# A two-layer hybrid decoder step: indexer keys loaded page by page by SyncE, K and V in one gather, weights and state laid out on the host

## The reference

```python
# per layer
z = h @ w_in                      # h = RMSNorm_pre(x); [q | k | v | indexer q | indexer k | head weights | pool input]
# indexer: relu(qi . ki) * wi, summed over 8 heads; the 256 (prompt: 128) best keys of each query stay
ki_past = cki[page_table].reshape(B, past, IDX_DIM)
_, sel = lax.top_k(sc, topk)
o = sparse_attend(q, k[sel], v[sel], valid)
p = pool(...)                     # running means over 2, 4, 8, 16 tokens, then a small matmul per group
x = x + RMSNorm_post(concat([o, p]) @ w_out)
x = x + RMSNorm_post(ConvGatedFFN(RMSNorm_pre(x)))     # gate and value 1024 x 2816, conv over 3 tokens, down
```

## Time and profile before

| | |
|---|---|
| median of 3 timed runs | 1708.46 us (1699.88 to 1721.88) |
| span of the profiled execution | 1881.7 us |
| PE busy | 1567.8 us, 83% |
| DVE, ACT, POOL busy | 45%, 26%, 14% |
| DMA | 116.45 MB, mean 62 GB/s |

### The profile page before, as it was taken

The page is one execution under the profiler, slowest core; times in us unless marked ns, Lnnn a source line. Parts: engine busy times, 40 slices in busy tenths (PEclk is TensorE's granted clock), DMA queues, the critical chain, the costliest instruction groups (busy, mean ns, idle before and its releaser), DMA issues.

```text
span 1881.7 us, 29237 instructions
## 1 busy us (share of the span) xinstructions
PE 1567.8 (83%) x10216; PEld 1330.8 (71%) x10216; DVE 850.0 (45%) x1731; ACT 482.0 (26%) x867; POOL 272.5 (14%) x260
## 2 busy tenths in 40 slices
PE   5369967748979999999862999766698999999996
PEld 3146644426969999999830758543487999998996
DVE  1003875624375555642210268753334655557221
ACT  4011301313342222332120132023234322224221
POOL 3710020150020000000176002004102000000002
PEclk8579977657989999999965996957678999999997
DMA  5112101010223333323311211011002233332331
GB/s 163 53 59 59 24 6 53 6 41 1 68 57 90 90 93 95 92 77 93 97 46 44 82 24 23 6 54 32 15 23 68 68 90 92 94 92 73 93 96 46
DMA packets 189622, 116.45 MB, mean 62 GB/s; under 512 B 25716, under 2 KB 184908, under 8 KB 189306
## 3 DMA queue, kind: packets, MB, share of 16 engines
q1 hardware_dynamic: 183246, 102.50, 19.7%
q0 software_dynamic: 6272, 12.63, 2.4%
HBM read 111.30 MB, written 4.44 MB: 62 GB/s over the span
## 4 chain that ended last, share of the span: by engine, by line
PE 72%; issue 12%; DVE 7%; ACT 3%; another core or an unknown queue 2%; DMA 1%; POOL 1%; DVEq 1%; SPq 0%; ACTq 0%; POOLq 0%
PE ps L740 44%; PE ps L725 6%; PE ps L765 4%; PE ps L837 3%; PE ps L984 2%; PE ps L1005 2%; PE ps L828 2%; PE ps L993 1%; POOL xT L620 1%; PE ps L854 1%; PE ps L712 1%; PE ps L788 1%; PE ps L1031 1%; DVE TS L1451 1%
## 5 line engine op out<-in xcount | busy, mean ns | idle before, releaser
L740 PE MATMUL ps<-moR_r,W_r 128*128 128x260 f32 x1408 | 284.8, 284 | 0.0
L740 PEld LDWEIGHTS ps<-moR_r,W_r 128*128 128x128 f32 x1408 | 219.0, 190 | 0.0
L620 POOL TENSOR_TENSOR xT<-xT,moR 128x520 f32<-128x520 f32 x32 | 45.6, 1462 | 1031.9 <-DVE moR L1468 1031.9
L740 PE MATMUL ps<-hT_r,QZC_r 128*128 128x260 f32 x896 | 183.9, 287 | 0.0
L725 PE MATMUL ps<-hT,W 128*128 128x260 f32 x576 | 163.4, 431 | 0.0
L765 PE MATMUL ps<-W,hT 128*128 128x328 f32 (+1 forms) x160 | 81.2, 609 | 94.5 <-issue 91.6
L740 PE MATMUL ps<-moR_r,QZC_r 128*128 128x260 f32 x704 | 148.5, 293 | 12.1 <-DVE hT_r L1810 11.8
L740 PE MATMUL ps<-moR_r,SQ_r 128*128 128x260 f32 x704 | 143.7, 285 | 0.0
L740 PEld LDWEIGHTS ps<-hT_r,QZC_r 128*128 128x128 f32 x896 | 142.4, 194 | 0.0
L740 PE MATMUL ps<-hT_r,SQ_r 128*128 128x260 f32 x704 | 141.4, 282 | 0.0
L765 PEld LDWEIGHTS ps<-W,hT 128*128 128x128 f32 (+1 forms) x160 | 33.4, 223 | 139.3 <-issue 129.4
(11 more groups left out here) (328 smaller groups left out, 3063.0 us busy)
## 6 DMA issues: line engine op xcount, KB each, us to landing
W<-in_w_gate SPq DMA_DIRECT2D x44, 512.0 KB, 3.9
W<-in_w_val SPq DMA_DIRECT2D x44, 512.0 KB, 3.9
W<-in_w_down SPq DMA_DIRECT2D x16, 1408.0 KB, 7.0
W<-in_w_in SPq DMA_DIRECT2D x8, 1024.0 KB, 5.6
W<-in_w_in SPq DMA_DIRECT2D x16, 256.0 KB, 4.2
W<-in_w_out SPq DMA_DIRECT2D x16, 256.0 KB, 4.1
W<-in_w_out SPq DMA_DIRECT2D x8, 512.0 KB, 5.1
yR<-in_x_prompt SPq DMA_DIRECT2D x1, 2048.0 KB
```

The costliest lines, as they stand in the source:

```text
L620: nc.gpsimd.tensor_tensor(xT[:, k, :], xT[:, k, :], mo[:, k, :], ALU.add).then_inc(x_ready.sem, 1)
L740: last = mm(ps[:, 2 * (g % 2) + f, 0:HT], w(k), x(k)[:, f * HT:(f + 1) * HT], start=(k == 0 and n == 0), stop=(k == nk - 1 and n == 2))
```

## The change

Indexer keys: the host lays the cache out as `idx_pages`, each page 64 dimensions by 128 keys. SyncE reads a page id from the page table in SBUF into a register and loads the page with a plain DMA (64 partitions by 128 floats). PE multiplies it directly; the page transposes on PE and the copies on ACT are gone, and so are POOL's 64 gathers per layer. K and V are one array `kv_rows` of 256 floats per row, fetched by 16 gathers per layer and not 32. Weights, x, y, the vectors and the convolution state are laid out by the host, so that each weight tile is one contiguous DMA and nothing is transposed at the start and the end. POOL copies the kept convolution columns in place of PE's transposes. The loop over the layers is written out.

```diff
-                wait_alone(sp, *so_ev(l, 0))
...
-                wait_alone(sp, *tile_done(l, 0))
-                load(0)
-                load(1)
+                if l:
+                    wait_alone(sp, *tile_done(l, 0))
+                    load(0)
+                    load(1)
+                with sp.Fori(0, NB) as b:
+                    for j in range(NPG):
+                        page = sp.value_load(PT[0:1, bass.ds(b, 1), j:j + 1], min_val=0, max_val=N_PHYS - 1)
+                        g = j % 2
+                        sp.dma_start(IK[64 * g:64 * g + 64, bass.ds(b, 1), j // 2, :],
+                                     A["idx_pages"][l, bass.ds(page, 1)].rearrange("o d r -> d o r")
+                                     ).then_inc(pages_in.sem, 16)
                 wait_alone(sp, *kv_mm(l, 5))
                 load(2)
```

```diff
             def layer(l):                                        # POOL
-                wait_alone(gp, *tile_done(l, 0))
-                for j in range(64):
-                    nc.gpsimd.indirect_dma_start(
-                        IK[:, j, :], None, page_pairs,
-                        bass.IndirectOffsetOnAxis(ap=idxI[:, j // NPP, j % NPP:j % NPP + 1], axis=0)
-                    ).then_inc(pages_in.sem, 16)
...
-                for dst, rows, s in ((KG, k_rows, kg_in), (VG, v_rows, vg_in)):
-                    for b in range(NB):
-                        for t in range(2):
-                            nc.gpsimd.indirect_dma_start(
-                                dst[:, 2 * b + t, :], None, rows,
-                                bass.IndirectOffsetOnAxis(ap=IDX[:, b, t:t + 1], axis=0)).then_inc(s.sem, 16)
+                for j in range(2 * NB):
+                    nc.gpsimd.indirect_dma_start(
+                        KVG[:, j, :], None, kv_rows,
+                        bass.IndirectOffsetOnAxis(ap=IDX[:, j // 2, j % 2:j % 2 + 1], axis=0)).then_inc(kg_in.sem, 16)
```

```diff
                 pe.wait_ge(*pages_in(l, 16 * NB * NPG))          # PE
-                for g in range(16):
-                    pe.wait_ge(*(dot_relu(l, 24) if g < 2 else pg_ev(l, g - 1)))
-                    for i in range(4):
-                        last = turn(ps[:, 4 + g % 2, i * P:(i + 1) * P], IK[:, 4 * g + i, :], ident)
-                    last.then_inc(pg_mm.sem, 1)
...
+                for b in range(NB):
+                    for j in range(NPP):
+                        q = NPP * b + j
+                        last = mm(ps[:, 6 + q // 32, 16 * (q % 32):16 * (q % 32) + 16], IK[:, b, j, :], qib[:, b, :],
+                                  start=True, stop=True)
+                    last.then_inc(sdot_mm.sem, 1)
```

```diff
-            for t in range(NT):
-                wait_alone(sp, *y_ev(0, 2 * t + 2))
-                sp.dma_start(O["y_prompt"][0, t * P:(t + 1) * P, :], x_rows[:, t, :]).then_inc(y_out.sem, 16)
+            for k in range(0, KD, 2):
+                wait_alone(sp, *x_ready(DEPTH, k + 2))
+                sp.dma_start(O["yT"][:, k:k + 2, :], xT[:, k:k + 2, :]).then_inc(y_out.sem, 16)
```

More of the change, by code:

```diff
@@ L744, in layer @@
             def layer(l):
-                pe.wait_ge(*vec_in(l, 16 * 9))
-                pe.wait_ge(*co_ev(l, 0))
-                turn(ps[:, 7, 0:124], vec_rows[0:124, :], ident[0:124, 0:124])
-                rows = NB * POOL_BUF
-                for g in range(4):
-                    mm(ps[:, 7, P + 8 * g:P + 8 * g + 8], state_rows[0:rows, g * P:(g + 1) * P],
-                       const("wsel", rows)[:, 8 * g:8 * g + 8], start=True, stop=True)
-                for i in range(NF):
-                    last = turn(ps[:, 6, 16 * i:16 * i + 16], conv_rows[:, i * P:(i + 1) * P], ident[0:16, 0:16])
-                last.then_inc(prep_mm.sem, 1)
                 arrived(l, 0)
@@ L900, in layer @@
                 pe.wait_ge(*rot_used(l, 8))
-                for g in range(4):
-                    turn(ps[0:15, 6, g * P:(g + 1) * P], XPb[:, g, 512:527], ident)
-                for g in range(4):
-                    last = turn(ps[0:NB, 7, g * P:(g + 1) * P], XS[:, g, :], ident)
-                last.then_inc(pout_mm.sem, 1)
                 arrived(l, 7)
@@ L1109, in layer @@
                 along_tokens(l, 3)
[L1111 removed]
+            for l in range(DEPTH):
                 layer(l)
[L1114 to L1123 removed]
         @block.scalar
         def _(act):
[L1128 removed]
+            for signal in (evac, so_ev):
                 act.sem_inc(signal.sem, 1)
@@ L1414, in layer @@
                 roots(l, 3)
-            with act.Fori(0, DEPTH) as l:
+            for l in range(DEPTH):
                 layer(l)
-            for n in range(10):
-                t, half = divmod(n, 2)
-                act.wait_ge(y_mm.sem, n + 1)
-                dst = x_rows[:, t, :] if t < NT else xs_rows
-                m = P if t < NT else NB
-                copy(dst[0:m, 512 * half:512 * half + 512], ps[0:m, n % 4, :]).then_inc(y_ev.sem, 1)
         @block.vector
@@ L1435, in _ @@
             dve.wait_ge(const_in.sem, 32)
-            for g in range(2):
-                r = slice(64 * g, 64 * g + 64)
-                ts(idxI[r, :, :], PT[r, :, g:NPG:2], 64.0, const("row64")[r], ALU.mult, ALU.add
-                   ).then_inc(tables.sem, 1)
             nc.vector.tensor_copy(phys[:, :, :, :], PT[:, :, :].rearrange("p b (j two) -> p two b j", two=2)
@@ new lines, in returned @@
+def returned(r):
+    rows = r["yT"].transpose(1, 0, 2).reshape(D_MODEL, TOK).T
+    pool_p = r["pool_rows"].transpose(0, 3, 2, 1).reshape(DEPTH, 1, POOL_BUF, 512)
+    last = r["pool_last"].transpose(0, 3, 2, 1).reshape(DEPTH, NB, 1, 512)
+    conv = r["conv_rows"].transpose(0, 3, 2, 1).reshape(DEPTH, 10, D_FF)
+    conv_s = np.stack([r["conv_kept"], conv[:, 2:]], axis=2)
+    return tuple(np.ascontiguousarray(x) for x in (
+        rows[None, :SEQ], rows[SEQ:, None], r["new_k_prompt"], r["new_v_prompt"], r["new_ik_prompt"], pool_p,
+        conv[:, None, 0:2], r["new_k_sample"], r["new_v_sample"], r["new_ik_sample"],
+        np.concatenate([r["pool_kept"], last], axis=2), conv_s))
```

346 lines of the change are left out of this document (147 added, 199 removed).

## The result

The changed kernel takes 1937.68 us (median of 4 runs, 1937.2 to 1943.35), the kernel before 1705.72 (4 runs, 1699.88 to 1721.88): a ratio of 1.1348, 95% interval 1.1292 to 1.1403. The forecast was 1900 us. The profiled execution of the change has a span of 1935.4 us, in agreement with its timed runs.

The account below looks back on a forecast made before the run. PE, busy 83% of the span, was taken as the engine whose stalls can be won back or added. 1708.5 + 207.7 + 4 - 20.8 = 1899.4, say 1900 us; range 1730 to 2010 us.

Parts of the forecast that it names:

- The price of a page: SyncE's time per page in its queue: DMA 0.30 plus five rows of 0.19, 1.25 us, 160 us per layer.
- The stall: PE waits for the third indexer-query tile, queued behind 128 pages: cost 106.7 us in layer 0, 101.0 in layer 1.
- What lies outside the stall: End, pool-output transposes, output weights and feed-forward transposes: gains summing to -20.8 us.
- The end: After the last addition PE no longer turns y back: -7.6 us.
- The page transposes: 64 on PE and 16 ACT evacuations per layer removed: 0 won, 1 us at most, since PE waits for DVE.
- The crawl: PE slowed beside POOL's gathers, matmuls 2.80 us apart: 184 us, taken to be in the profiled execution, not timed ones.
- Hidden pages: Rival: pages under about 0.4 us, SP done before PE's second tile, no stall: 1666 us; chance 0.05.
- The real crawl: Rival: timed runs pay the crawl too, removal returns 154 us: 1745 us at 1.25 us per page; chance 0.11.
- The first rival: Cheap pages in SP's queue, hidden before PE's second tile: 1708.5 - 21 - 21 = 1666 us; chance 0.05.
- the 21 us for earlier starts: Removed start transposes: 14 us in layer 0, some 7 in layer 1, won only if SP is not last.
- The dearer load: Rival: register load on SyncE as long as POOL's issue, 0.95 us, page 2.0 us: 2092 us; chance 0.08.
- The line T = 1580 + 256 X: Forecast time of the whole kernel by page price X in SP's queue: 0.8 gives 1785 us, 1.6 gives 1990.

Follow-up runs that it names:

- second profile: The kernel before, unchanged, profiled again: 1709.09 us (8 runs), ratio 0.9999, span 1702.2 us.
- The kernel with GpSimd's gathers: The changed kernel with SyncE's page loop removed; GpSimd gathers the host-turned pages by 64 indirect DMAs per layer: 1667.34 us, ratio 0.9725 to the kernel before.

## Why the prediction was right

**The place was right.** The page loop in SP's queue, load(2) behind it and PE's third indexer-query tile waiting for it are what the chain and the waits show, and the wait that was measured (266.4 us) is, but for 3 us, the whole difference of the spans to the kernel in which the pages alone were moved (269.6). The feed-forward stage stayed full, as forecast.

**The price of a page was too low.** Forecast 1.25 us, measured 1.41 and 1.49. The term that was off is the DMA's issue: taken at 0.30 from the earlier trace rows, it was 0.50 for this form. Load and register rows were put at 5 x 0.19 = 0.95 and came to 0.91 in layer 0 (0.99 in layer 1). The load took 0.27 us. The Trainium skill's 600 ns ("DMA: Bandwidth & Descriptors", section "Latency and other measured facts"), by which the forecast would have been 2004 us, is not what this case shows. The page loops took 180.3 and 190.1 us, not 160 each: together 50 us more than forecast, which is more than the 38 us by which the whole forecast was low.

**The stall, by its own sum.** Layer 0: load(2) landed and PE started at 204.94, forecast 184.2; the kernel before starts at 84.22 and not at the 77.5 of the prediction. That makes 120.7 for 106.7. Layer 1: 1158.72 - 961.59 = 197.1 for 166.6, against 913.39 - 848.41 = 65.0 before, where 65.6 was reckoned: 132.1 for 101.0. Sum 252.8 for 207.7, 45 too little. The slower start of PE was put at 4 us: the first group behind the stall took 9.48 us in layer 0 and 8.76 in layer 1, where such a group at full clock takes 7.01, so 4.2 (in layer 0 of the kernel before it took 7.57).

**What lies outside the stall** came to -20 us: the spans, 1935.4 against 1702.2 of the undisturbed profile of before, are 233.2 apart, less 252.8. Forecast was -20.8 + 4 = -17. That the sums are near is luck in part, for the terms are not:

- The end, forecast -7.6: after the last addition to `xT` the kernel before takes 10.7 us (1691.5 to 1702.2), the changed one 3.3 (1932.1 to 1935.4), so -7.4.
- The output weights as one DMA, forecast -2 per layer: from the start of PE's output projection to that of the feed-forward products it took 83.2 and 82.5 us before and takes 82.1 each, so -1.1 and -0.4.
- The transposes in the feed-forward stage, forecast -5 for both layers: the same products took 245.1 us in each layer with the 22 transposes among them and take 243.5, so -1.6 per layer and -3.2 in all.
- A term that the prediction didn't have: PE's wait between the gate and value products and the down projection fell from 4.8 to 3.2 us per layer. The prediction held that the new layout could win nothing in this stage. Whether the layout of the weights is the cause was not tried.
- The page transposes, forecast 0, and the pool-output transposes, forecast -2.1 per layer, are below.

The feed-forward products of layer 1 in the chains, first before (from 1296.14 to 1541.27), then in the change:

```profile
1296.14 1.63 PE ps L740 x12
...
1529.76 11.51 PE ps L740 x96
```

```profile
1538.56 243.52 PE ps L694 x2028
```

**The page transposes** are the step where a reading failed. They were put at 0, from PE's 10.88 us of wait for DVE behind the stage in layer 0 and DVE's 19.10 busy of 20 in layer 1. In layer 0 of that execution the stage ran at full clock, and PE was done early. In layer 1 of the same execution the clock fell to 0.50 within the stage, PE was late itself, and its wait for DVE was 1.41 us, in a row that the prediction leaves out; DVE's busy time did not say which of the two was late. Both layers of the second profile are like that layer 1 (0.55, 1.42 us). The rows of the first profile:

```profile
200.00:233.00 33.00, 32.24 (x228) 26.30 (x228) 30.10 (x78) 13.96 (x29) 1.66 (x2) 1.00 0.18 33
...
1163.62 0.62 PE L876 MATMUL ps<-C,sTok 128*64 128x128 f32 x2 [1.41 <-DVE snew L1597]
```

From the last small matmuls before the stage to the picks, the kernel before takes 34.8 us in the layer at full clock (210.75 to 245.54) and 41.6 and 40.8 in the second profile. The change takes 33.6 and 33.7, at a clock of 0.56 in layer 0. So the removal is worth 8.0 and 7.2 us against the second profile, where the clock falls. Where it stays full, the two numbers (34.8 and 33.6) say about 1, close to the prediction's 0; no run compares the two there. The kernel with GpSimd's gathers wins the same there, and 17 us of time in all (1684.47 against 1667.34). The two ends of the stage, in the second profile of before and in the change:

```profile
155.49 0.43 PE L847 MATMUL ps<-wdiag,C 8*128 8x64 f32 x2
...
311.78 0.61 PE L812 MATMUL ps<-C,sTok 128*64 128x128 f32 x2 [2.97 <-DVE snew L1485]
```

The first is the start before (its end, 197.06, is shown above), the second the end in the change (its start is 278.19).

In the change some of that is lost again: from the picks to the output projection it takes 192.3 and 191.6 us, the kernel before 189.8 and 188.7, though its pool-output transposes are gone. No run here shows why.

**The crawl.** Read as a thing of the profiled execution, from two numbers that agreed (184 us of excess, 173 between span and median). The two profiles of the kernel before are 179.5 us apart (1881.7 and 1702.2). The second profile confirms it, and so does the change, whose timed runs show nothing like the 154 us that a real crawl would have given back. The part of the reading that failed is that the gathers make it: I forecast it for every profiled kernel that gathers at the start, and none of the four others that do so showed it.

**The rivals.** Hidden pages would have needed a page below 0.4 us: the page was 1.4, and even without a lookup 0.84. The real crawl is excluded by the second profile. The first rival's 1666 us, which the kernel with GpSimd's gathers meets at 1667, is a sum of terms that cancel: of the 21 us for earlier starts, the 14 in layer 0 came (third tile at 70.33 for 84.01) and the 7 in layer 1 did not (told at the end of this section), while the page transposes, put at 0, gave 17. The dearer load did not come, 0.27 us. The line T = 1580 + 256 X gives 1951 at the measured mean of 1.45 (measured 1937.7) and 1795 at 0.84 (measured 1782.1): the slope is right, and both are 13 us too high.

**What the change is worth in parts**, by timed medians: layouts, merge and the new start and end 1709 to 1684; page transposes 1684 to 1667; the pages in SP's queue 1667 to 1938. The first two are a gain of 42 us. They are to be had with the pages left on GpSimd, which is the version that beats both kernels (1664 to 1667 us).

Part of a gain can be lost on the way too. In layer 1 the K/V projection of the version with GpSimd's gathers starts 10.5 us after the first slot is free, where the kernel before needs 16.0. But the third tile stands 66.3 us after that point, against 65.0. The timelines of the projection, that version and then the kernel before:

```profile
833.37 5.12 PE L711 MATMUL ps<-W,hT 128*128 128x328 f32 x8 [3.17 <-ACT hT L1070]
...
847.16 7.28 PE L711 MATMUL ps<-W,hT 128*128 128x328 f32 x16
```

```profile
864.43 6.59 PE L765 MATMUL ps<-W,hT 128*128 128x328 f32 x12 [1.11 <-ACT hT L1158]
...
874.93 4.68 PE L765 MATMUL ps<-W,hT 128*128 128x328 f32 x16
```

The same pass takes 7.28 us for 4.68. The granted clock was 0.62 from 833 to 847 us and 0.82 from 847 to 862; in the kernel before it was 0.72 from 864 to 875 and 1.00 from 875 to 913. So the start won is gone again at the lower clock. Why the clock came back later here was not tried. In layer 0 the 14 us were won in full.

## What to carry to other kernels

A DMA whose address comes from a register costs the issuing queue its whole row of work: lookup, check and address arithmetic, with the gaps between them, were two thirds of 1.41 us here. Multiply by the count, and then look at what is queued behind, before moving an indirect gather to a plain queue; 64 gathers of 1.25 us on an idle GpSimd made PE wait for nothing, 128 pages of 1.41 us on the queue of the weights cost 270 us.

When the span of a profile is far from the timed median, price the disturbance and profile the kernel once more if you can. And read a wait in every layer, with the granted clock beside it: the same wait of PE for DVE was 10.88 us in layer 0 of one execution, at full clock, and 1.41 in layer 1, at half clock. A term of 0 drawn from the one was 8 us in the other.

## What was not expected of the hardware

- The same kernel, with the same gathers, was profiled at 1881.7 us and at 1702.2 us. In the slow one PE's matmuls stood 2.80 us apart for over 50 us in each layer.
- Issuing a DMA of 64 partitions of 512 bytes took SP 0.50 us, one of 128 partitions of 512 bytes with a simpler pattern 0.35, and a small one of the earlier trace rows 0.30.
- The granted clock fell in a stage in which PE is busy nearly all the time. In the products of query block and pages (128 rows at 16 columns each, x128) the stretch shows PE busy 27.29 of 31.90 us at a mean granted clock of 0.55, and the record of a matmul lasts 0.37 us against 0.18 at its fastest in the kernel before. Transposes between the products did not bring the clock back there (0.55 too). But it does not always fall: in layer 0 of the first profile of the kernel before, the whole stage with its transposes ran at 1.00. What decides it was not tried. First the kernel without the transposes, then with them, columns as in the earlier trace rows:

```profile
143.00:174.90 31.90, 27.29 (x135) 26.18 (x136) 31.68 (x88) 0.00 (x0) 0.87 (x3) 0.55 0.07 30
```

```profile
141.00:182.80 41.80, 39.63 (x201) 38.21 (x201) 33.23 (x93) 10.81 (x24) 1.72 (x2) 0.55 0.08 26
```
